# Three-product latent keys and values, and a weight unit shared between two engines inside the norms

## The chip, the core and the metric

One core of a Trainium2 chip runs the whole program. The metric is the device time of one execution in microseconds. In one core, TensorE (PE) multiplies, with its weight loads shown as PEld; VectorE (DVE), ScalarE (ACT) and GpSimd (POOL) work elementwise; SyncE (SP) issues most DMAs. PE writes PSUM, which has eight banks of 128 x 512 floats here; POOL works on SBUF alone.

## The reference

512 tokens of width 1024 pass through two layers of a first block and then one layer of a second block, all in float32. A layer of the first block projects x with `w_in` and mixes three groups: a gated recurrence, latent attention and attention to a memory. The latent group is

```
q = (_rmsnorm(cq, q_norm) @ w_uq).reshape(B, S, MLA_HEADS, MLA_NOPE + MLA_ROPE)
c = _rmsnorm(ckv, kv_norm)
k_nope = (c @ w_uk).reshape(B, S, MLA_HEADS, MLA_NOPE)
v = (c @ w_uv).reshape(B, S, MLA_HEADS, MLA_VDIM)
k_rope = _rope(kr, cos, sin)
```

with c of 512 x 128 and `w_uk`, `w_uv` of 128 x 512. The layer ends with `x = _layernorm(DEEPNORM_ALPHA * x + y, ln_g[l], ln_b[l])`. The second block is a chain of branches, each of the form `h = h + rms_norm(f(rms_norm(h, pre_g)), post_g)`: a feed-forward (SwiGLU, width 2816), a mixer (neighbourhood attention and pooling), a second feed-forward, and a last gated projection. Where one branch ends and the next begins, an outer norm and the next inner norm follow each other.

## The kernel before

**Split products.** Nearly every matrix product in float32 is made as three products of the shorter type `fp32r`. A factor w is split into `wh` (the high part, a cast to fp32r) and `wl = w - wh` (the low part), and PE adds `wh*xh`, `wh*xl` and `wl*xh` in one PSUM bank (L882 to L884).

**Units.** The weights come in 128-row tiles, four tiles to a unit. A `Block` of eight tiles has two units, and its pieces (unit, bank j) are PE's work, in this order: unit 0 with banks 0 to 3, then unit 1 with banks 0 to 3. For a unit, SP loads `raw` (two buffers, L812), ACT casts each tile to `wh` (three buffers, L1226, in `prepare`), and POOL subtracts to `wl` (L831). `low_on_dve(u, k)` says which tiles DVE subtracts instead (L1631, in `low`): every second one of the first eight units. SP loads a unit when the low parts of the unit two before are made. ACT casts a unit when its load has landed and PE is done with the unit three before. PE waits for tile k's low part at each unit's bank 0.

**Norms.** `norm_order` writes out by hand the order of each engine's steps over the four token tiles t, for the five norms between blocks. Four have an inner gain (`pre`) too: behind layer 1 of the first block (mode `layer`), behind the first feed-forward, the mixer and the second feed-forward (mode `post`). In these, per tile: the last partial products are added by DVE (`evac`; L1610), the outer gain is multiplied in (`gain`, L1952 or L1948), ACT makes the mean square and its root (`root`, L1491 and L1492), DVE finishes x (`x`, L1963 or L1960), ACT makes the second mean square and root (`root2`, L1498 and L1499), DVE multiplies by its reciprocal and by the inner gain in two halves (`n`, L1971), PE transposes the tile (`turn`, L1128), ACT casts it (`high`, L1509, or L1506 behind the first feed-forward), and DVE subtracts (`low`, L1987 or L1981). PE fills its time with the last pieces of the branch (`part`) and, from the first two transposed tiles, with the first halves of the next block's pieces: `early[0]`, transposes of tile 2, `early[1]`, transposes of tile 3, `early[2]`. `lots` cuts these pieces in three: for a block of eight such pieces 2, 4, 2 in mode `post` and 4, 2, 2 in mode `layer`; behind the second feed-forward there are four pieces (full width, half of the banks), cut 1, 2, 1. `early[0]` waits for `high(1)` and `low(1)`. ACT's casts of the next block's units stand in its order as `units`: unit 0 at the start of the norm, unit 1, all four tiles, behind `root2(2)` and before `root(3)` in mode `post` (behind `root2(2)` in mode `layer` too).

**Latent part.** `latent_norm` normalizes cq and ckv; `latent_turn` transposes them (L961), and ACT writes the high part `ch` of the queries' input, the whole c (`c_t`) and the rotary key (L1348 to L1352); DVE writes the low part of the queries' input (L1776). Behind it PE makes what is left of a gate block and the two blocks of `w_uq`, whose outputs DVE takes with L1596, and then the keys (L970) and values (L976): per layer four products each of plain float32, 128 x 128 by 128 x 512. ACT copies half of each key bank (L1368), then spreads the rotary key over the second half of the heads (L1362, L1363), and PE's first attention score (L991) waits for it. `w_uk` and `w_uv` are loaded whole beforehand.

Of the kernel before, what the change touches and what calls it, by code (L numbers as in the profile page):

```python
# [220 lines left out]
def norm_order(first, pre, turned):  # L221
# [9 lines left out]
    else:  # L231
# [17 lines left out]
        if first == "layer":  # L249
# [13 lines left out]
            def root(t):  # L263
# [5 lines left out]
            dve += [n(3), low(2), low(3)] if pre else [low(2), low(3)]  # L269
            act = [root(0), root2(0), [("units", 0)], root(1), high(0), root2(1), root(2), high(1), root2(2),  # L270
                   [("units", 1)], root(3), root2(3), high(2), high(3)]
        else:
            pe = parts[:5] + [turn(0), parts[5], parts[6], turn(1), parts[7], early[0], turn(2), early[1], turn(3), early[2]]
            act, dve = [[("units", 0)]], []
            for t in range(T):
# [13 lines left out]
    free = ("part", "early", "evac", "units")  # L289
# [4 lines left out]
def build(nc, x, x_t, mem_t, positions, w_in, w_uq, w_uk, w_uv, w_mk, w_mv, w_out, ln_g, ln_b, cols_in,  # L294
# [3 lines left out]
    with ctx:  # L298
# [24 lines left out]
        with nc.sbuf_tensor("work", [P, work_n], F32) as work:  # L323
            pass
        work2 = sb("work2", [P, work2_n])
# [35 lines left out]
        c_t, uk, uv = area(4224, 512), area(4736, 512), area(5248, 512)  # L361
# [100 lines left out]
        for l in range(DEPTH):  # L462
# [57 lines left out]
            add(latent_turn)  # L520
            add(between)
# [199 lines left out]

        def low_on_dve(u, k):

            return u < 8 and k % 2 == 1
# [111 lines left out]
        def _(pe):  # L836
# [63 lines left out]
            for e in plan:  # L900
# [67 lines left out]
                elif e.kind == "latent_keys":  # L968
                    for p in range(4):
                        pe.matmul(ps[:, 4 + p, :], uk[:, p * P:(p + 1) * P], c_t, start=True, stop=True).then_inc(pe_step, 1)  # L970
                elif e.kind == "latent_values":
                    for t in range(T):
# [3 lines left out]
                        pe.matmul(ps[:, 4 + t, :], c_t[:, t * P:(t + 1) * P], uv, start=True, stop=True).then_inc(pe_step, 1)  # L976
# [120 lines left out]
                elif e.kind == "norm":  # L1097
# [4 lines left out]
                    lots = early[:first], early[first:3 * n], early[3 * n:]  # L1102
# [83 lines left out]
        def _(act):  # L1186
# [23 lines left out]
            def prepare(pc, whole=False):  # L1210
# [4 lines left out]
                share = -(-units[last][2] * (j + 1) // b.banks)  # L1215
# [50 lines left out]
            for e in plan:  # L1266
# [77 lines left out]
                elif e.kind == "latent_turn":  # L1344
                    for n in range(4):
# [3 lines left out]
                        elif n == 2:  # L1349
                            ins = act.activation(c_t, ps[:, 6, :], ACT.Copy, scale=col("kv_gain", e.layer))  # L1350
                        else:
                            ins = act.copy(k_rope, ps[:, 7, :])  # L1352
                        ins.then_inc(act_step, 1)
                elif e.kind == "rope_table":
# [110 lines left out]
                elif e.kind == "norm":  # L1465
# [699 lines left out]
```

## Time and profile before

| | us |
|---|---|
| median of 3 runs | 2126.18 |
| lowest and highest | 2125.7, 2127.97 |
| the profiled execution's own time | 2127.59 |
| its span, first to last instruction | 2125.8 |
| PE busy (share of the span) | 2093.5 (98%) |
| PE weight loads busy | 1736.8 (82%) |
| DVE busy | 900.6 (42%) |
| POOL busy | 884.2 (42%) |
| ACT busy | 788.8 (37%) |

A busy engine has an instruction in flight. Matmuls overlap, so PE's progress is read from the distance between their starts and not from the length of one. The granted TensorE clock is 0.999 of full speed over the span.

### The profile page before, as it was taken

Reading aid. Unit: us, or ns where it says so; the run is one execution under the profiler, and the core shown is the slowest. Engines: PE = TensorE matmul, PEld = TensorE weight load, DVE = VectorE, ACT = ScalarE, POOL = GpSimd, SP = SyncE. Lnnn points to the kernel's source line nnn. Section 1 sums busy time; section 2 is a strip of 40 time slices with the busy share of each in tenths; the row PEclk is TensorE's granted clock in tenths of the full one; section 3 lists DMA queues with packets and bytes.
Section 4 is the critical chain, followed back from the end, with each engine's and each line's share of the span. In section 5 each row is a group of like instructions: output and inputs, shape, how many; then the busy total and the mean of one; then the engine's idle time right before and its main releaser. Section 6 shows DMA issues by size and latency. Waiting matters only on the chain.

```text
span 2125.8 us, 33452 instructions
## 1 busy us (share of the span) xinstructions
PE 2093.5 (98%) x13804; PEld 1736.8 (82%) x13804; DVE 900.6 (42%) x1639; ACT 788.8 (37%) x1607; POOL 884.2 (42%) x688
## 2 busy tenths in 40 slices
PE   7999999999999999999999999999999999999998
PEld 7888887778978887778888888888888888888876
DVE  6273565535373565526432221533422612222264
ACT  4424335454423325555422222335423432222244
POOL 4643433232543434233454444343445345444433
PEclk9999999999999999999999999999999999999999
DMA  6522223122222223122242332242232233332222
GB/s 234 180 74 80 77 67 100 41 80 80 80 82 80 77 67 99 40 80 76 72 140 89 110 99 93 76 134 80 76 103 99 62 109 101 106 116 87 96 70 89
DMA packets 98680, 196.65 MB, mean 93 GB/s; under 512 B 3681, under 2 KB 12257, under 8 KB 98145
## 3 DMA queue, kind: packets, MB, share of 16 engines
q1 hardware_dynamic: 95072, 183.25, 26.4%
q10 hardware_dynamic: 3456, 11.27, 1.5%
q8 instruction: 109, 1.79, 0.3%
q14 instruction: 43, 0.34, 0.1%
HBM read 192.41 MB, written 2.10 MB: 91 GB/s over the span
## 4 chain that ended last, share of the span: by engine, by line
PE 62%; DVE 5%; ACT 1%; issue 0%; DVEq 0%
PE ps L882 19%; PE ps L883 19%; PE ps L884 19%; DVE work L1971 1%; DVE xs L1963 1%; PE ps L991 1%; DVE work L1952 1%; PE ps L1068 1%; PE ps L999 0%; PE ps L1008 0%; PE ps L1151 0%; DVE side L1610 0%; PE ps L1171 0%; ACT work L1498 0%; DVE xl L1987 0%
## 5 line engine op out<-in xcount | busy, mean ns | idle before, releaser
L831 POOL TENSOR_TENSOR wl<-raw,wh 128x512 fp32r<-128x512 f32 (+2 forms) x684 | 884.0, 1317 | 1216.7 <-ACT wh L1226 1207.1
L1226 ACT CAST wh<-raw 128x512 fp32r<-128x512 f32 (+2 forms) x692 | 380.3, 603 | 772.0 <-PE ps L884 667.8
L882 PE MATMUL ps<-xh,wh 128*128 128x512 f32 (+1 forms) x1376 | 514.0, 374 | 1.2 <-issue 1.2
L884 PE MATMUL ps<-xh,wl 128*128 128x512 f32 (+1 forms) x1376 | 508.9, 370 | 0.0
L883 PE MATMUL ps<-xl,wh 128*128 128x512 f32 (+1 forms) x1376 | 508.4, 369 | 0.0
L882 PEld LDWEIGHTS ps<-xh,wh 128*128 128x128 f32 x1376 | 259.3, 188 | 46.1 <-issue 3.9
L884 PEld LDWEIGHTS ps<-xh,wl 128*128 128x128 f32 x1376 | 259.0, 188 | 44.6
L883 PEld LDWEIGHTS ps<-xl,wh 128*128 128x128 f32 x1376 | 259.3, 188 | 42.1
L882 PE MATMUL ps<-wh,xh 128*128 128x512 f32 (+1 forms) x608 | 239.0, 393 | 0.2 <-issue 0.2
L884 PE MATMUL ps<-wh,xl 128*128 128x512 f32 (+1 forms) x608 | 234.3, 385 | 0.0
L883 PE MATMUL ps<-wl,xh 128*128 128x512 f32 (+1 forms) x608 | 234.3, 385 | 0.0
L882 PE MATMUL ps<-wh,yh 128*128 128x512 f32 x496 | 198.1, 399 | 2.3 <-POOL wl L831 2.2
L884 PE MATMUL ps<-wh,yl 128*128 128x512 f32 x496 | 193.5, 390 | 0.0
L883 PE MATMUL ps<-wl,yh 128*128 128x512 f32 x496 | 193.3, 390 | 0.0
L1614 DVE TENSOR_TENSOR work<-ps,work 128x512 f32<-128x512 f32 x44 | 30.3, 688 | 380.6 <-PE ps L884 380.6
L882 PEld LDWEIGHTS ps<-wh,xh 128*128 128x128 f32 x608 | 114.1, 188 | 22.7 <-issue 1.3
L884 PEld LDWEIGHTS ps<-wh,xl 128*128 128x128 f32 x608 | 114.1, 188 | 21.8
L883 PEld LDWEIGHTS ps<-wl,xh 128*128 128x128 f32 x608 | 114.2, 188 | 20.3 <-issue 0.2
L882 PEld LDWEIGHTS ps<-wh,yh 128*128 128x128 f32 x496 | 93.3, 188 | 22.8 <-issue 2.8
L884 PEld LDWEIGHTS ps<-wh,yl 128*128 128x128 f32 x496 | 93.1, 188 | 20.0
L883 PEld LDWEIGHTS ps<-wl,yh 128*128 128x128 f32 x496 | 93.2, 188 | 18.4
L1610 DVE TENSOR_TENSOR side<-side,ps 128x512 f32<-128x512 f32 x88 | 59.3, 686 | 106.0 <-PE ps L884 103.4
(261 smaller groups left out, 2430.6 us busy)
## 6 DMA issues: line engine op xcount, KB each, us to landing
raw<-w_in SPq DMA_DIRECT2D x58, 1024.0 KB, 5.2
raw<-w_out SPq DMA_DIRECT2D x20, 1024.0 KB, 5.1
raw<-f1g SPq DMA_DIRECT2D x10, 1024.0 KB, 5.1
raw<-f1u SPq DMA_DIRECT2D x10, 1024.0 KB, 5.1
raw<-f1d SPq DMA_DIRECT2D x10, 1024.0 KB, 5.0
raw<-f2g SPq DMA_DIRECT2D x10, 1024.0 KB, 5.1
raw<-f2u SPq DMA_DIRECT2D x10, 1024.0 KB, 5.1
raw<-f2d SPq DMA_DIRECT2D x10, 1024.0 KB, 5.1
```

Of the source, the lines that this page charges most:

```text
L831: pool.tensor_tensor(wl[s], raw[:, u % 2, k, 0:b.width], wh[s].bitcast(F32), ALU.subtract).then_inc(low_done, 1)
L882: pe.matmul(o, still[0], move[0], start=k0 + k == 0, stop=False)
L883: pe.matmul(o, still[0], move[1], start=False, stop=False)
L884: mm = pe.matmul(o, still[1], move[0], start=False, stop=k0 + k == b.ktiles - 1)
L991: mm = pe.matmul(ps[:, 4 + h, 0:width], q_heads[:, 2 * p + h, cut], k_heads[:, p, h, 0:width], start=True, stop=True)
L1068: mm = pe.matmul(ps[o:o + 32, 4 + h, at:at + n], K[:, h, own:own + 32], right, start=True, stop=True)
L1226: act.copy(wh[:, v % 3, k, 0:width], raw[:, v % 2, k, 0:width]).then_inc(high_done, 1)
L1610: ins = dve.tensor_copy(dst, src) if first else dve.tensor_tensor(dst, dst, src, ALU.add)
L1614: link(dve.tensor_tensor(tmp, src, SG[:, j, :], ALU.mult))
L1952: step_done(dve.tensor_tensor(normed[:, t, :], facc[:, t, :], gain2_b[:, 0, :], ALU.mult))
L1963: step_done(dve.scalar_tensor_tensor(out=xt, in0=normed[:, t, :], scalar=r, in1=xt, op0=ALU.mult, op1=ALU.add))
L1971: step_done(dve.scalar_tensor_tensor(out=dst, in0=xs[:, t, cut], scalar=stat[:, 28 + t:29 + t], in1=gain2_b[:, 1, cut] if e.gain == "work2 ...
```

## The change

In the four norms with an inner gain, the second unit of the next block is treated in halves. ACT casts tiles 0 and 1 behind `high(1)` and before `root2(2)`, and tiles 2 and 3 behind `root(3)`. The low parts of tiles 2 and 3 go from POOL to DVE, in its order as `unit_low`, behind `x(3)`; in mode `post`, `low(2)` goes from behind `x(3)` to behind `n(3)`. Where the next block has eight early pieces, they are cut 2, 3, 3 (`post`) or 3, 2, 3 (`layer`).

In the latent part, a step `latent_split` behind `latent_turn` splits c, `w_uk` and `w_uv`: ACT writes the high parts, DVE the low ones (`uk_l` and `uv_l` in place of the raw weights). Keys and values become three fp32r products each.

```
-            dve += [n(3), low(2), low(3)] if pre else [low(2), low(3)]
-            act = [root(0), root2(0), [("units", 0)], root(1), high(0), root2(1), root(2), high(1), root2(2),
-                   [("units", 1)], root(3), root2(3), high(2), high(3)]
+            if pre:
+                dve += [[("unit_low", 0)], n(3), low(2), low(3)]
+                act = [root(0), root2(0), [("units", 0)], root(1), high(0), root2(1), root(2), high(1), [("units", 1)],
+                       root2(2), root(3), [("units", 2)], root2(3), high(2), high(3)]
+            else:
+                dve += [low(2), low(3)]
+                act = [root(0), [("units", 0)], root(1), high(0), root(2), high(1), [("units", 2)], root(3), high(2),
+                       high(3)]
...
-                if t:
+                if 0 < t < last:
                     dve.append(low(t - 1))
-                act.append([("units", 1), ("root", t)] if t == last else [("root", t)])
+                act.append([("root", t)])
+                if t == last:
+                    act.append([("units", 2)])
                 if t:
                     act.append(high(t - 1))
+                if t == last - 1:
+                    act.append([("units", 1)])
                 act.append(root2(t))
-            dve += [n(last), low(last)]
+            dve += [[("unit_low", 0)], n(last), low(last - 1), low(last)]
...
+            add(Phase("latent_split", act=2, dve=3, layer=l, free_running=True))
...
-            return u < 8 and k % 2 == 1
+            return k % 2 == 1 if u < 8 else u in shared_lows and k >= 2
...
-                        pe.matmul(ps[:, 4 + p, :], uk[:, p * P:(p + 1) * P], c_t, start=True, stop=True).then_inc(pe_step, 1)
+                        cut = slice(p * P, (p + 1) * P)
+                        pe.matmul(ps[:, 4 + p, :], uk_h[:, cut], c_h, start=True, stop=False)
+                        pe.matmul(ps[:, 4 + p, :], uk_h[:, cut], c_l, start=False, stop=False)
+                        pe.matmul(ps[:, 4 + p, :], uk_l[:, cut], c_h, start=False, stop=True).then_inc(pe_step, 1)
...
-                        pe.matmul(ps[:, 4 + t, :], c_t[:, t * P:(t + 1) * P], uv, start=True, stop=True).then_inc(pe_step, 1)
+                        cut = slice(t * P, (t + 1) * P)
+                        pe.matmul(ps[:, 4 + t, :], c_h[:, cut], uv_h, start=True, stop=False)
+                        pe.matmul(ps[:, 4 + t, :], c_h[:, cut], uv_l, start=False, stop=False)
+                        pe.matmul(ps[:, 4 + t, :], c_l[:, cut], uv_h, start=False, stop=True).then_inc(pe_step, 1)
...
-                    lots = early[:first], early[first:3 * n], early[3 * n:]
+                    second = 3 * n
+                    if e.gain and n == 2:
+                        first, second = 3 if e.mode == "layer" else 2, 5
+                    lots = early[:first], early[first:second], early[second:]
...
-                            if t < len(e.slots[1]):
-                                prepare(e.slots[1][t], whole=True)
+                            if e.tiles and t == 1:
+                                prepare(e.slots[1][1], upto=2)
+                            elif t < 3:
+                                prepare(e.slots[1][min(t, 1)], whole=True)
...
+                elif e.kind == "latent_split":
+
+                    act.wait_ge(small_loaded, e.loads_before)
+                    act.wait_ge(pe_step, e.pe)
+                    act.copy(uk_h, uk).then_inc(act_step, 1)
+                    act.copy(uv_h, uv).then_inc(act_step, 1)
...
+                elif e.kind == "latent_split":
+
+                    dve.wait_ge(act_step, e.act - 1)
+                    step_done(dve.scalar_tensor_tensor(out=c_l, in0=ps[:, 6, :], scalar=col("kv_gain", e.layer),
+                                                       in1=c_h.bitcast(F32), op0=ALU.mult, op1=ALU.subtract))
+                    for n, (low_part, whole, high_part) in enumerate(((uk_l, uk, uk_h), (uv_l, uv, uv_h))):
+                        dve.wait_ge(act_step, e.act + n + 1)
+                        step_done(dve.tensor_tensor(low_part, whole, high_part.bitcast(F32), ALU.subtract))
...
+                        elif key[0] == "unit_low":
+                            for k in (2, 3):
+                                low(e.next_block.unit_ids[1], k)
```

## Rows read from the trace of the kernel before

**Rows 1.** The page: span, and busy time of each engine

```profile
span 2125.8 us, 33452 instructions
...
PE 2093.5 (98%) x13804; PEld 1736.8 (82%) x13804; DVE 900.6 (42%) x1639; ACT 788.8 (37%) x1607; POOL 884.2 (42%) x688
```

**Rows 2.** PE's waits, whole span: us in total, times, longest

```profile
PE ps L1128 <- DVE work L1971: 5.9, 8, 1.2
```

**Rows 3.** Timeline of PE, mixer's norm: start, length, idle before

```profile
1691.00 0.36 PE L882 MATMUL ps<-xh,wh 128*128 128x256 f32 x1 [0.35 <-issue]
...
1693.94 0.60 PE L1128 MATMUL ps<-ident,work 128*128 128x128 f32 x4
1695.39 0.66 PE L1128 MATMUL ps<-ident,work 128*128 128x128 f32 x4 [0.85 <-DVE work L1971]
1695.80 0.36 PE L882 MATMUL ps<-xh,wh 128*128 128x256 f32 x1
...
1702.35 1.32 PE L1128 MATMUL ps<-ident,work 128*128 128x128 f32 x8 [0.55 <-DVE work L1971]
1703.42 0.36 PE L882 MATMUL ps<-xh,wh 128*128 128x256 f32 x1
```

**Rows 4.** Timeline of DVE, the same stretch

```profile
1688.42 1.28 DVE L1963 SCALAR_TENSOR_TENSOR xs<-work,stat,xs 128x1024 f32<-128x1024 f32 x1
...
1692.33 3.01 DVE L1971 SCALAR_TENSOR_TENSOR work<-xs,stat,work 128x512 f32<-128x512 f32 x2
1695.26 2.29 DVE L1952 TENSOR_TENSOR work<-side,work 128x1024 f32<-128x1024 f32 x1
...
1697.66 2.13 DVE L1963 SCALAR_TENSOR_TENSOR xs<-work,stat,xs 128x1024 f32<-128x1024 f32 x1
...
1701.54 1.42 DVE L1971 SCALAR_TENSOR_TENSOR work<-xs,stat,work 128x512 f32<-128x512 f32 x2
```

**Rows 5.** Timeline of ACT, the same stretch

```profile
1687.29 1.22 ACT L1509 CAST xh<-ps 128x512 fp32r<-128x512 f32 x2 [0.25 <-PE ps L1128]
1689.74 1.06 ACT L1498 ACTIVATE work<-xs 128x1024 f32<-128x1024 f32 x1 [1.23 <-DVE xs L1963]
...
1691.12 2.17 ACT L1226 CAST wh<-raw 128x512 fp32r<-128x512 f32 x4
...
1699.83 1.06 ACT L1498 ACTIVATE work<-xs 128x1024 f32<-128x1024 f32 x1 [3.16 <-DVE xs L1963]
```

**Rows 6.** Timeline of POOL, the same stretch

```profile
1691.80 6.91 POOL L831 TENSOR_TENSOR wl<-raw,wh 128x512 fp32r<-128x512 f32 x4 [18.57 <-ACT wh L1226]
```

**Rows 7.** By line: ns minimum/median/maximum, first and last start

```profile
L1971 DVE SCALAR_TENSOR_TENSOR work<-xs,stat,work x24: 744/752/1771, 1374.8 to 2070.2; 128x512 f32<-128x512 f32 x24
...
L1631 DVE TENSOR_TENSOR wl<-raw,wh x16: 683/1344/1781, 7.0 to 52.7; 128x512 fp32r<-128x512 f32 x16
...
L831 POOL TENSOR_TENSOR wl<-raw,wh x684: 724/1292/3210, 6.6 to 2099.9; 128x512 fp32r<-128x512 f32 x155, 128x256 fp32r<-128x256 f32 x12, 128x416 fp32r<-128x416 f32 x4
```

**Rows 8.** Timelines of PE and of its loads, layer 1's latent part

```profile
841.88 0.39 PE L884 MATMUL ps<-zh,wl 128*128 128x512 f32 x1
842.11 3.59 PE L970 MATMUL ps<-work 128*128 128x512 f32 x8
845.54 3.60 PE L976 MATMUL ps<-work 128*128 128x512 f32 x8
848.97 0.61 PE L991 MATMUL ps<-work 128*128 128x128 f32 x4
...
848.54 0.19 PEld L991 LDWEIGHTS ps<-work 128*128 128x128 f32 x1 [0.24 <-ACT work L1363]
```

**Rows 9.** Timeline of ACT, the same stretch

```profile
845.74 0.58 ACT L1368 COPY work<-ps 64x512 f32<-64x512 f32 x1 [0.28 <-PE ps L970]
```

**Rows 10.** Timeline of ACT and DVE behind the latent transposes

```profile
827.07 0.65 ACT L1226 CAST wh<-raw 128x512 fp32r<-128x512 f32 x1
...
832.57 0.69 DVE L1596 TENSOR_TENSOR work<-ps,rope_table 128x512 f32<-128x512 f32 x1 [5.96 <-PE ps L884]
```

More of the change, by code:

```diff
@@ L279, in norm_order @@
                 dve.append([("gain", t), ("x", t)])
-                if t:
+                if 0 < t < last:
                     dve.append(low(t - 1))
-                act.append([("units", 1), ("root", t)] if t == last else [("root", t)])
+                act.append([("root", t)])
+                if t == last:
+                    act.append([("units", 2)])
                 if t:
                     act.append(high(t - 1))
+                if t == last - 1:
+                    act.append([("units", 1)])
                 act.append(root2(t))
-            dve += [n(last), low(last)]
+            dve += [[("unit_low", 0)], n(last), low(last - 1), low(last)]
             act.append(high(last))
         pe, act, dve = (sum(order, []) for order in (pe, act, dve))
-    free = ("part", "early", "evac", "units")
+    free = ("part", "early", "evac", "units", "unit_low")
     at = [{k: i + 1 for i, k in enumerate(k for k in order if k[0] not in free)} for order in (pe, act, dve)]
@@ L324, in build @@
             pass
+        with nc.sbuf_tensor("front", [P, 2560], F32):
+            with nc.sbuf_tensor("latent_parts", [P, 3, 512], F32R) as latent_parts:
+                with nc.sbuf_tensor("middle", [P, 128], F32):
+                    with nc.sbuf_tensor("latent_lows", [P, 3, 512], F32R) as latent_lows:
+                        pass
         work2 = sb("work2", [P, work2_n])
@@ L360, in build @@
         ch, cl = zh[:, 0:2, :], zh[:, 2:4, :]
-        c_t, uk, uv = area(4224, 512), area(4736, 512), area(5248, 512)
+        uk, uv = area(4736, 512), area(5248, 512)
+        c_l, uk_h, uv_h = (latent_parts[:, i, :] for i in range(3))
+        c_h, uk_l, uv_l = (latent_lows[:, i, :] for i in range(3))
         q_heads, k_heads, k_rope = area(6144, 8, 512), area(10496, 4, 2, 512), area(B, 512)
@@ L720, in build @@
                     written[e.writes] = tuple(step)
+        shared_lows = {e.next_block.unit_ids[1] for e in plan
+                       if isinstance(e, Phase) and e.kind == "norm" and e.tiles and e.gain}
         def low_on_dve(u, k):
-            return u < 8 and k % 2 == 1
+            return k % 2 == 1 if u < 8 else u in shared_lows and k >= 2
         low_at, low_upto, lows = {}, [(0, 0)], [0, 0]
@@ L1208, in _, with prepare @@
             ahead = [2, 0]
-            def prepare(pc, whole=False):
+            def prepare(pc, whole=False, upto=None):
                 b, unit, j = pc
@@ L1214, in prepare @@
                 last = min(u, len(units) - 1)
-                share = -(-units[last][2] * (j + 1) // b.banks)
+                share = upto or -(-units[last][2] * (j + 1) // b.banks)
                 while ahead[0] <= last:
@@ L1349, in _ @@
                         elif n == 2:
-                            ins = act.activation(c_t, ps[:, 6, :], ACT.Copy, scale=col("kv_gain", e.layer))
+                            ins = act.activation(c_h, ps[:, 6, :], ACT.Copy, scale=col("kv_gain", e.layer))
                         else:
```

## The prediction

> **What bounds the kernel now.** I read the page first: TensorE (PE) is busy 2093.5 of 2125.8 us [rows 1]. So a saving must be PE time, either matmuls that get shorter or stretches in which PE waits. The second view is who PE waits for. In the whole span its matmuls wait 5.9 us, in eight waits, for L1971, which makes the twice-normed tile that PE transposes next [rows 2]. The eight are two in each of the four norms with an inner gain. Third, the timeline of one of them, the norm behind the mixer, engine by engine. PE starts `early[0]` at 1691.00 and the first transpose of token tile 2 at 1693.94. The second one comes only at 1695.39, after 0.85 us idle. `early[1]` runs from 1695.80, and tile 3's transposes start at 1702.35 after 0.55 us idle [rows 3]. VectorE (DVE) shows why. Its L1971 pair takes 3.01 us at 1692.33 but 1.42 at 1701.54. The product L1952 takes 2.29 us and L1963 2.13 at 1697.66, while L1963 took 1.28 at 1688.42 [rows 4]. GpSimd (POOL) subtracts four low parts from 1691.80 for 6.91 us, exactly over these slow ones [rows 6], released by four casts of ScalarE (ACT) at 1691.12 [rows 5]. Over all its uses L1971 has a median of 752 ns and a maximum of 1771 [rows 7]. POOL and DVE delay each other when both read two operands from SBUF.
>
> For the latent part I read PE's timeline of layer 1. Keys (L970) start at 842.11 and values (L976) at 845.54, four plain f32 products each, and the first attention score follows at 848.97. A split product of the same 512 columns starts 0.23 us before its successor (841.88 to 842.11) [rows 8].
>
> **The norms, part by part** (times of the mixer's norm).
>
> ACT: of the four casts of the next block's second unit, two move ahead of `root2(2)`, two behind `root(3)`. The `high(1)` casts run from 1687.29 for 1.22 us and end at 1688.5; `root2(2)` began only at 1689.74, since it waits for L1963, which ends at 1689.70 [rows 4, 5]. Two casts cost 2 x 0.54 (2.17 over 4) = 1.1 us and end at 1689.6, so they are hidden in the idle time. The weight buffer that they overwrite is free once piece (3,0) is done, which stands before tile 1's transposes in PE's order and so before `high(1)`. Their load waits only for low parts of earlier units, and POOL has been idle for 18.57 us before 1691.80 [rows 6], so it landed long before. `root(3)` no longer has four casts ahead of it: it starts at about 1692.1, when tile 3 has been added, and ends at 1693.6 (a square and root take about 1.55 us: ACT starts at 1699.83, DVE's next pair at 1701.54 less a 0.2 us reciprocal [rows 4, 5]). The other two casts end at 1694.7, and DVE asks for them only after `x(3)`.
>
> POOL: two subtractions instead of four. In the trace it starts 0.68 us after the casts do (1691.12 to 1691.80), so now at about 1689.1, while L1963 still runs. Either it waits until 1689.70 and works to about 1692.3 (two at the median of 1292 ns [rows 7]), or L1963 is stretched. The fast L1963 of 1.28 us beside a slow one of 2.13 [rows 4] leaves at most 0.85 us for that. I take no stretch: the slow L1971 of 1771 ns is its 744 plus 1.03 us, one whole stay behind POOL and not twice the speed lost, so the one already running keeps its place [rows 7].
>
> The Trainium skill, "SBUF — State Buffer", section Terms, says of the port pair that both engines use that it is exclusive and held for the full instruction, and that the loser fully blocks and doesn't share bandwidth. By that, L1963 keeps 1.28 us and my sum stands; by a shared bandwidth it would be up to 0.85 us longer in each norm and 3.4 us would be lost. The steps of one size in the trace agree with the rule.
>
> DVE: `n(2)` runs 1692.33 to 1693.75 instead of to 1695.3, because POOL is done. L1952 then takes 1.2 and L1963 1.28 us: `x(3)` ends at 1696.5 instead of 1699.8. The two moved subtractions cost 683 ns each, the fast case of the same subtraction in L1631 [rows 7]: 1.4 us, ending at 1697.9. They lie inside the wait for `root2(3)`, 1.55 us, after which `n(3)` runs from 1698.3 to 1699.7. `low(2)` moves behind `n(3)` and costs nothing: its reader is the second half of the block, after `early[2]`. If POOL got in between, each would cost up to 1781 ns [rows 7], 3.6 us for both, and `n(3)` would be 2.0 us later.
>
> PE: `early[0]` keeps two of eight pieces and ends at 1693.94 as before; the second transposes of tile 2 find `n(2)` ready. Both halves take about 1.0 us (1702.35 to 1703.42 for tile 3, without a wait between). `early[1]` now has three pieces, 36 products at 0.12 us (24 took 1691.00 to 1693.94 [rows 3]), so 4.4 us, to 1699.4. Its third piece needs the second unit's low parts in turn: it starts at about 1697.9 and its third product group 0.7 us later, against DVE's 1697.2 and 1697.9 for these two. That fits narrowly. Tile 3's second half is ready at 1699.7, a wait of 0.2 or so; `early[2]` has three pieces from 1700.2 to 1704.6. Before, it had two from 1703.42 to 1706.4. That is 1.8 us less. The other norms differ in the count: behind layer 1 the split is 3, 2, 3 instead of 4, 2, 2, behind the second feed-forward it stays 1, 2, 1. Their waits are of the same size (5.9 over 4 = 1.48 each, here 0.85 + 0.55 = 1.40). I take 1.7 x 4 = 6.8 us. Bounds: from 5.9 less 4 x 0.3 left over = 4.7, to 4 x 2.0 = 8.0.
>
> **The latent products.** PE now does 24 split products per layer for 8 plain ones: 24 x 0.234 = 5.6 us against 848.97 - 842.11 = 6.86. That is 1.24 us per layer of PE alone. But the first score waits for ACT's last spread of the rotary key. That chain is: last key product, 0.20 us, the copy L1368 at 845.74 [rows 9], then two spreads. PE's load for the score was released by the second one (L1363) at 848.54 [rows 8], which is where PE arrived anyway, with values from 845.54 at 0.43 us a load. The chain shortens only by the keys' part, 3.43 - 12 x 0.234 = 0.62 us. So the load comes at 847.92, and without a queued product ahead of it the product follows in about 0.2 instead of 0.43 us, at 848.1: 0.85 us won per layer, 1.7 in two. Bounds 1.2 (0.62 x 2) and 2.5 (1.24 x 2).
>
> The Trainium skill, "FP8 and Floating Point Precision", section TensorE Precision Notes, has true FP32 as four passes. Three for four would take a quarter off 6.86, 1.7 us a layer, against 1.24 by the trace, where a plain product takes 0.86 and three split ones 0.70.
>
> The splitting itself: two ACT copies (0.54 each) behind L1352, and three DVE subtractions (0.7 each, up to 1.8 beside POOL). DVE then waits 5.96 us until 832.57 for PE, so even 5.3 us would be covered. ACT has the cast at 827.07 behind it, 1.1 us later; it belongs to the second block of w_uq, which PE reads behind the whole first one, whose first output DVE takes at 832.57, so it is covered too [rows 10]. No DMA is added: the raw weights are loaded as before.
>
> **Sum.** 6.8 + 1.7 = 8.5 us from the profiled execution's 2127.59. Its span is 2125.8 and some 1.8 us lie around it; the median is 2126.18, 1.4 us under the profiled one, and I set the prediction against the median: 2126.2 - 8.5 = 2117.7 us. Everything behind a norm is paced by PE, so the time won is not given back there; the loads behind the norms start as much earlier.
>
> **Rivals.**
> (a) DVE takes on what POOL loses: the moved subtractions come late (slow beside POOL, or `root2(3)` is sooner than thought). Then only the first waits of each norm go, some 0.8 us x 4, plus 1.7: 4.9 us, 2121.3. For it: 1.4 us in a gap of 1.55 is tight. Against: POOL has nothing left to do there.
> (b) POOL's earlier start stretches L1963, and `low(1)`, on which `early[0]` waits at 1691.00, comes late by up to 0.85 us: 3.4 us lost, 5.1 won, 2121.1.
> (c) The latent part gains the full PE time or nothing, at 2116.9 or 2119.4: inside the range.
> (d) The other side: `early[1]` now holds a piece that needs the low parts which DVE makes last, behind `x(3)`, and `n(3)` stands behind them in the same queue. Each microsecond by which these are late beyond about 0.2 is paid by PE in all four norms. At 2.1 us late the norms' gain is gone; at 3.4 us late the kernel is 4 x 3.2 - 8.5 = 4.3 us slower, 2130.5. What would do it: casts held up in ACT's queue behind `root(3)`. Against: 1.8 us lie between the casts' end and `x(3)`.
> (e) It does nothing, since the waits are replaced by others one step on (`low(3)` before the second half): 2124.5 with the latent part alone. Against: `low(3)` gets 4.4 us of cover instead of 2.9.
>
> **Chances.** My forecast with (c) 0.70, (a) 0.09, (b) 0.09, (e) 0.08, (d) 0.04. A change of 0.2% is 4.25 us, about what a measurement of this kernel can tell from none. Faster by more: 0.70 + most of (a) and (b), 0.86; within: 0.11; slower: 0.03. The range reaches from 2115.7 (8.0 + 2.5) to 2121.9, which takes in (a) and (b).
>
> **What the profile of the changed kernel would show.** L1971 without any instance near 1771 ns in the norms, and at most 0.3 us of PE waits on it per norm; L1963 of tile 2 at 1.28 us (1.6 or more speaks for (b)); two subtractions of 0.68 us on DVE between `x(3)` and `n(3)`; keys at 2.8 us and values at 2.8 us, the score's load released by ACT's spread. PE waits on low parts inside `early[1]` would make (d) or (a) right and me wrong.

## The result and the profile after

The changed kernel takes 2114.88 us (median of 4 runs, 2114.51 to 2117.76), beside 2126.24 us (4 runs) for the kernel before on the same chip: a ratio of 0.9943, interval 0.9931 to 0.9955. The forecast was 2117.7 us with a range of 2115.7 to 2121.9. The direction was right. The gain is 11.4 us where 8.5 were forecast, and the time lies 0.8 us below the range.

The page of the changed kernel (span, busy time of each engine), and PE's waits over the whole span (us in total, times, longest):

```profile
span 2113.3 us, 33496 instructions
...
PE 2089.2 (99%) x13820; PEld 1741.6 (82%) x13820; DVE 894.8 (42%) x1653; ACT 789.8 (37%) x1611; POOL 868.0 (41%) x680
```

```profile
PE ps L902 <- POOL wl L851: 8.6, 2, 7.9
PE ps L1094 <- DVE work L1943: 2.6, 2, 1.3
PE ps L902 <- issue: 1.4, 4, 0.4
```

The eight waits for the twice-normed tile [rows 2] are gone altogether. PE's busy time went from 2093.5 us [rows 1] to 2089.2. Of these 4.3 us the latent parts gave 2.3. Up to the gated recurrence of layer 0 PE was 0.8 us busier, and most of the rest is time in which PE had stood still in the norms inside rows that count as busy (shown below). (In the changed kernel L902 to L904 are the split products, L1157 the norm's transposes, L2019 the twice-normed tile, L2000 the gain product, L2011 what `x` makes, L851 and L1668 the low parts on POOL and DVE, L1255 the weight casts.)

The mixer's norm on PE (start, length, then the idle time before, if any). It answers to [rows 3]:

```profile
1682.90 0.35 PE L902 MATMUL ps<-xh,wh 128*128 128x256 f32 x1 [0.35 <-issue]
...
1685.85 1.03 PE L1157 MATMUL ps<-ident,work 128*128 128x128 f32 x8
1686.64 0.36 PE L902 MATMUL ps<-xh,wh 128*128 128x256 f32 x1
...
1691.03 1.03 PE L1157 MATMUL ps<-ident,work 128*128 128x128 f32 x8
1691.82 0.36 PE L902 MATMUL ps<-xh,wh 128*128 128x256 f32 x1
```

Eight transposes now run as one row of 1.03 us, and the next product starts 0.79 us behind their start. Before, tile 2's were torn into 0.60, a wait and 0.66, and tile 3's came late and had a length of 1.32, with the next product 1.07 us behind their start. The same stretch on DVE, to be read beside [rows 4]:

```profile
1680.32 1.28 DVE L2011 SCALAR_TENSOR_TENSOR xs<-work,stat,xs 128x1024 f32<-128x1024 f32 x1
...
1684.23 1.41 DVE L2019 SCALAR_TENSOR_TENSOR work<-xs,stat,work 128x512 f32<-128x512 f32 x2
1685.56 1.22 DVE L2000 TENSOR_TENSOR work<-side,work 128x1024 f32<-128x1024 f32 x1
...
1686.89 1.28 DVE L2011 SCALAR_TENSOR_TENSOR xs<-work,stat,xs 128x1024 f32<-128x1024 f32 x1
1688.09 1.29 DVE L1668 TENSOR_TENSOR wl<-raw,wh 128x512 fp32r<-128x512 f32 x2
1689.72 0.17 DVE L2017 RECIPROCAL stat<-stat 128x1 f32<-128x1 f32 x1 [0.34 <-ACT stat L1536]
1689.92 1.41 DVE L2019 SCALAR_TENSOR_TENSOR work<-xs,stat,work 128x512 f32<-128x512 f32 x2
```

and on ACT and POOL, to be read beside [rows 5, 6]:

```profile
1680.31 1.14 ACT L1255 CAST wh<-raw 128x512 fp32r<-128x512 f32 x2
...
1685.41 1.12 ACT L1255 CAST wh<-raw 128x512 fp32r<-128x512 f32 x2
```

```profile
1681.01 3.01 POOL L851 TENSOR_TENSOR wl<-raw,wh 128x512 fp32r<-128x512 f32 x2 [15.53 <-ACT wh L1255]
```

The slow pair of L1971 (3.01 us) is now 1.41, the gain product 1.22 instead of 2.29, the second L2011 1.28 instead of 2.13. POOL starts its two at 1681.01, while the first L2011 runs; that one keeps its 1.28 us, and POOL has done at 1684.02, just ahead of L2019 at 1684.23. The two subtractions on DVE take 1.29 us and end 0.34 us before the root that `n(3)` waits for arrives.

The latent part of layer 1 on PE and on its weight loads, beside [rows 8]. Keys are L991 to L993, values L1000 to L1002, the score L1017:

```profile
841.86 0.39 PE L993 MATMUL ps<-latent_lows 128*128 128x512 f32 x1
842.08 0.39 PE L1000 MATMUL ps<-latent_parts,latent_lows 128*128 128x512 f32 x1
...
844.58 0.39 PE L1002 MATMUL ps<-latent_parts 128*128 128x512 f32 x1
845.06 0.71 PE L1017 MATMUL ps<-work 128*128 128x128 f32 x4
845.53 0.48 PE L902 MATMUL ps<-wh,yh 128*128 128x512 f32 x1
```

```profile
845.06 0.52 PEld L1017 LDWEIGHTS ps<-work 128*128 128x128 f32 x4 [0.52 <-ACT work L1398]
```

Each split product stands 0.227 us behind the one before. Between the last value product and the score lie 0.48 us, and PE's load waited 0.52 us for ACT's second spread (L1398). From the first key product (839.36) to the product behind the score it is now 6.17 us; before it was 7.23 (842.11 to 849.34).

**Where the time came from, by stages.** Starts of the same instruction in both profiled executions (2127.59 and 2115.07 us, 12.5 us apart):

- Up to the first matmul of the gated recurrence in layer 0 (line L1068 before, L1094 after; the "first level matmul" from here on), 106.36 before and 104.56 after: 1.8 us. Nothing of the change runs before it. The experiments below have this start anywhere from 104.31 to 107.83, so this is no part of the gain.
- The latent parts: 1.06 us in layer 1 and 0.95 in layer 0 (here from its first key product to layer 1's: 361.54 to 842.11 before, 359.74 to 839.36 now), 2.0 together. Up to the product behind the score layer 0 gains 1.06 too; 0.11 goes again between there and layer 1.
- The norms. From `early[0]`'s first product to the first behind tile 3's transposes it was 1691.00 to 1703.42, 12.42 us, and now it is 1682.90 to 1691.82, 8.92. One piece of 12 products (1.44 us) has moved behind that point, so the gain is 3.50 - 1.44 = 2.06 us. The same sum gives 2.06 behind layer 1 and 1.90 behind the first feed-forward; behind the second, where the cut didn't change, it is 2.42 outright. Together 8.4 us.

- Between the first feed-forward's norm and the mixer's: 0.38 us (1399.14 to 1691.00 before, 1389.98 to 1682.90 less the piece of 1.44 now). Of this, 0.35 lie at one place, the transposes of tile 0 in the mixer's norm. They start 0.43 us behind PE's last product, where it is 0.23 now, and the next product comes 0.98 us behind their start, where it is 0.83. DVE was late with the tile: its reciprocal before the tile began 0.45 us behind the end of ACT's root, and now begins 0.10 behind it. The other stretches give 0.1 back.

Behind the start-up that makes 10.7 us. The 11.4 between the medians are 0.7 more.

### The profile page after: what moved, and what is told of

Same layout as the page of the kernel before. It is cut to its first block, busy times and chain, and to the rows that moved or that the text cites. A ratio compares the mean times of both kernels' runs of the same rounds, so it can differ in the third digit from the quotient of the medians.

```text
span 2113.3 us, 33496 instructions
## 1 busy us (share of the span) xinstructions
PE 2089.2 (99%) x13820; PEld 1741.6 (82%) x13820; DVE 894.8 (42%) x1653; ACT 789.8 (37%) x1611; POOL 868.0 (41%) x680
## 4 chain that ended last, share of the span: by engine, by line
PE 59%; ACT 1%; DVE 0%; issue 0%; DVEq 0%
PE ps L902 18%; PE ps L903 18%; PE ps L904 18%; PE ps L1017 1%; PE ps L1157 1%; PE ps L1025 0%; PE ps L1034 0%; PE ps L1180 0%; PE ps L1200 0%; PE ps L1189 0%; PE ps L1070 0%; PE ps L1052 0%; ACT L1581 0%; PE ps L974 0%; PE ps L1210 0%; PE ps L1062 0%
## 5 line engine op out<-in xcount | busy, mean ns | idle before, releaser
L851 POOL TENSOR_TENSOR wl<-raw,wh 128x512 fp32r<-128x512 f32 (+2 forms) x676 | 867.8, 1307 | 1220.6 <-ACT wh L1255 1210.8
L1255 ACT CAST wh<-raw 128x512 fp32r<-128x512 f32 (+2 forms) x692 | 380.7, 604 | 773.3 <-PE ps L904 672.8
L902 PE MATMUL ps<-xh,wh 128*128 128x512 f32 (+1 forms) x1376 | 514.2, 374 | 1.2 <-issue 1.2
L904 PE MATMUL ps<-xh,wl 128*128 128x512 f32 (+1 forms) x1376 | 509.1, 370 | 0.0
L902 PEld LDWEIGHTS ps<-xh,wh 128*128 128x128 f32 x1376 | 259.4, 189 | 46.1 <-issue 3.9
L904 PEld LDWEIGHTS ps<-xh,wl 128*128 128x128 f32 x1376 | 259.1, 188 | 44.6
L902 PE MATMUL ps<-wh,xh 128*128 128x512 f32 (+1 forms) x608 | 239.1, 393 | 0.2 <-issue 0.2
L904 PE MATMUL ps<-wh,xl 128*128 128x512 f32 (+1 forms) x608 | 234.4, 386 | 0.0
L902 PE MATMUL ps<-wh,yh 128*128 128x512 f32 x496 | 198.0, 399 | 0.2
L904 PE MATMUL ps<-wh,yl 128*128 128x512 f32 x496 | 193.6, 390 | 0.0
L902 PEld LDWEIGHTS ps<-wh,xh 128*128 128x128 f32 x608 | 114.2, 188 | 22.6 <-issue 1.4
L904 PEld LDWEIGHTS ps<-wh,xl 128*128 128x128 f32 x608 | 114.2, 188 | 21.8
L902 PEld LDWEIGHTS ps<-wh,yh 128*128 128x128 f32 x496 | 93.3, 188 | 20.5 <-POOL wl L851 0.8
L904 PEld LDWEIGHTS ps<-wh,yl 128*128 128x128 f32 x496 | 93.1, 188 | 19.9
```

The lines of the kernel that those rows point to most:

```text
L851: pool.tensor_tensor(wl[s], raw[:, u % 2, k, 0:b.width], wh[s].bitcast(F32), ALU.subtract).then_inc(low_done, 1)
L902: pe.matmul(o, still[0], move[0], start=k0 + k == 0, stop=False)
L904: mm = pe.matmul(o, still[1], move[0], start=False, stop=k0 + k == b.ktiles - 1)
L1255: act.copy(wh[:, v % 3, k, 0:width], raw[:, v % 2, k, 0:width]).then_inc(high_done, 1)
```

## The experiments

Because the start-up varies by more than some of the questions, each kernel is read in two ways: by its median against the kernel before, and by the **time behind the start-up**, that is, the profiled execution's time less the start of its first level matmul. For before this is 2127.59 - 106.36 = 2021.23 us, for the changed kernel 2115.07 - 104.56 = 2010.51. The last column is the difference to 2021.23. What the column can't take off is a change of the granted clock behind the start-up, which matters for e5.

| kernel | median us | ratio to before (interval) | profiled - start | behind the start-up |
|---|---|---|---|---|
| changed | 2114.88 | 0.9943 (0.9931 to 0.9955) | 2115.07 - 104.56 | -10.7 |
| e8, changed again | 2115.45 | 0.9947 (0.9934 to 0.9959) | 2116.08 - 105.43 | -10.6 |
| e1, norms alone | 2118.93 | 0.9959 (0.9945 to 0.9972) | 2118.93 - 105.88 | -8.2 |
| e2, latent part alone | 2124.57 | 0.9988 (0.9979 to 0.9997) | 2123.49 - 104.45 | -2.2 |
| e3, casts moved, POOL keeps its low parts | 2120.06 | 0.9964 (0.9952 to 0.9977) | 2121.62 - 107.31 | -6.9 |
| e4, low parts shared, casts in the old place | 2121.18 | 0.9971 (0.9961 to 0.9982) | 2122.32 - 105.94 | -4.9 |
| e5, spread ahead of the keys | 2121.57 | 0.9975 (0.9966 to 0.9984) | 2124.63 - 107.83 | -4.4 |
| e6, old cut of the early pieces | 2115.45 | 0.9951 (0.9938 to 0.9964) | 2115.28 - 104.31 | -10.3 |
| e7, all four low parts on DVE | 2117.58 | 0.9957 (0.9943 to 0.9971) | 2118.49 - 105.71 | -8.5 |
| e9, spread pair by pair | 2114.01 | 0.9940 (0.9926 to 0.9953) | 2114.40 - 104.64 | -11.5 |
| e10, e9's edit on before | 2128.41 | 1.0004 (0.9995 to 1.0014) | 2128.56 - 107.44 | -0.1 |

The kernel before had medians of 2127.1 us beside e1 to e4, 2126.47 beside e5 to e8 and 2126.09 beside e9 and e10. e8 says what the last column is good to: 0.1 to 0.2 us for one and the same code, while the starts of the two profiles differ by 0.87.

**e1 and e2: the two halves of the change apart.** e1 has the norms as changed and the keys and values as plain products, with their splitting taken out. e2 is the reverse.

> The change without its latent part: keys and values are plain f32 products again. Theory: all that PE waited in the four norms is gone, 2.06 + 1.90 + 2.06 + 2.42 = 8.4 us by the starts in the two traces, so about 2117.8 us. Rival (the prediction's own term): the norms give 6.8 us and the rest came from elsewhere, 2119.4.

> The latent part alone, norms as before. Theory: 1.0 us less in each layer, 2.0 in all, 2124.2 us; keys to first score takes 5.9 us instead of 6.86, the last 0.5 of it a wait for the rotary spread. Rival: the first stage of the program, where the changed kernel's trace was 1.8 us ahead, belongs to the change (another memory layout), then 3.5 us or more, 2122.7.

Measured: 8.2 and 2.2 us behind the start-up, together 10.4 of 10.7. The halves add up, and the norms are the one that was underrated: e1 fits the 8.4 by starts and not the rival's 6.8. In e2, against its rival, what lies behind the start-up is 2.2 us and not 3.5. PE's waits in e2 still have the row of before, to the digit:

```profile
PE ps L1145 <- DVE work L2005: 5.9, 8, 1.2
```

So 5.9 us of waits stand there, and taking them away brings 8.2 to 8.4. PE's waits in this table don't hold the whole stall. The same table has them once more as the weight loads see them (the kernel before):

```profile
PEld ps L1128 <- DVE work L1971: 9.4, 15, 1.4
```

In the changed kernel's trace 0.4 us of these 9.4 are left, in two waits at tile 1 of the mixer's norm. A load takes its wait where it happens. PE's idle time is counted only from the end of the last product's row, and that row is 0.28 us long where the next product could follow in 0.12.

**e3 and e4: which of the two moves does it.** e3 leaves the casts where the change puts them and gives the two low parts back to POOL:

```
-            return k % 2 == 1 if u < 8 else u in shared_lows and k >= 2
+            return u < 8 and k % 2 == 1
```

e4 keeps DVE's share and puts the four casts back together (and the same for the norm behind layer 1):

```
-                act.append([("root", t)])
-                if t == last:
-                    act.append([("units", 2)])
+                act.append([("units", 2), ("root", t)] if t == last else [("root", t)])
...
-                if t == last - 1:
-                    act.append([("units", 1)])
```

> The changed kernel, but POOL makes all four low parts of the second unit; ACT's order stays as changed. Theory (the two engines block each other at SBUF): POOL's third low part starts before x(3) and x(3) waits for it, n(3) is 0.9 us later in each norm, 3.6 us in all, 2118.5 us. Rival (all of the gain is that ACT's casts no longer stand ahead of root(3)): as the changed kernel, 2114.9.

> The changed kernel, but ACT casts all four tiles behind root2(2) and before root(3), as before; DVE still makes two low parts. Theory: POOL's two low parts start 2.7 us later and fall on n(2), and root(3) is 1.0 us later, so the first wait of each norm comes back, some 0.9 to 1.5 us each, 2118.5 to 2121 us. Rival (only the number of low parts on POOL counts): as the changed kernel, 2114.9.

Measured behind the start-up: e3 loses 3.8 us of the change's 10.7, e4 loses 5.8. With the 2.2 us of the latent part taken off, the casts' place alone is worth 4.7 us, DVE's share alone 2.7, both 8.4: they add up to a little less than the whole. In e3 it is tile 3's stall that comes back, in three of the four norms (behind the second feed-forward PE doesn't wait). POOL's second pair falls on `x(3)` (timelines of DVE and POOL, mixer's norm), and PE waits for the tile:

```profile
1692.21 2.13 DVE L2010 SCALAR_TENSOR_TENSOR xs<-work,stat,xs 128x1024 f32<-128x1024 f32 x1
...
1696.08 1.42 DVE L2018 SCALAR_TENSOR_TENSOR work<-xs,stat,work 128x512 f32<-128x512 f32 x2
```

```profile
1691.42 4.08 POOL L851 TENSOR_TENSOR wl<-raw,wh 128x512 fp32r<-128x512 f32 x2 [2.09 <-ACT wh L1255]
```

In e4 tile 2's stall comes back in all four norms. The four casts run as a block at 1687.46, POOL starts its two at 1688.14, just ahead of the twice-normed tile, and this is 3.01 us long again (timelines of DVE and PE):

```profile
1688.66 3.01 DVE L2015 SCALAR_TENSOR_TENSOR work<-xs,stat,work 128x512 f32<-128x512 f32 x2
```

```profile
1691.73 0.66 PE L1153 MATMUL ps<-ident,work 128*128 128x128 f32 x4 [0.84 <-DVE work L2015]
...
1696.42 0.28 PE L900 MATMUL ps<-xh,wl 128*128 128x256 f32 x1
1696.76 1.32 PE L1153 MATMUL ps<-ident,work 128*128 128x128 f32 x8
1697.83 0.36 PE L898 MATMUL ps<-xh,wh 128*128 128x256 f32 x1
```

A smaller part of tile 3's stall is back too, in three norms. Here it is 0.22 us ahead of the transposes (0.34 behind the last product instead of 0.12) and 0.28 inside them, since the late tile 2 makes tile 3 late. So each half of the move takes away mainly one stall, and the two are not quite independent. The slow gain product of before (2.29 us) comes back in neither: POOL's two subtractions are over when it starts (1.22 us in e3, 1.21 in e4).

**e6 and e8: is the new cut of the early pieces worth anything?** e6 is the changed kernel with the old cut, and e8 the changed kernel again.

```
-                    second = 3 * n
-                    if e.gain and n == 2:
-                        first, second = 3 if e.mode == "layer" else 2, 5
-                    lots = early[:first], early[first:second], early[second:]
+                    lots = early[:first], early[first:3 * n], early[3 * n:]
```

> The changed kernel with the early pieces cut as before (2, 4, 2 and 4, 2, 2). Theory: n(3) is ready 0.1 us ahead of the end of a three-piece early[1]; with four pieces it is ready sooner still, and what is lost is only cover for low(3) behind the last transposes, 2.9 us against about 2.1 needed: no difference, 2114.9. Behind layer 1, early[0] with four pieces hides more, so none is lost there either. Rival: the new cut is part of the gain, 0.3 us or more a norm, 2116.

> The changed kernel itself, beside the others on the same chip: a ratio near 0.9943 to the kernel before. Its first 104 us tell how far the start of the program differs by itself from one execution to the next.

Both have a median of 2115.45 us, and e6 is 0.3 us behind e8 by the last column, hardly more than that column's own error. The cut gives nothing that can be measured. Its third piece of `early[1]`, on which rival (d) rested, never waited in any norm of the changed kernel.

**e7: does DVE have room for all four low parts?**

```
-            return k % 2 == 1 if u < 8 else u in shared_lows and k >= 2
+            return k % 2 == 1 if u < 8 else u in shared_lows
...
-                            for k in (2, 3):
+                            for k in range(4):
```

> The changed kernel, but DVE makes all four low parts of the second unit, all between x(3) and n(3). Theory: two fit into the 1.55 us for which DVE waits for root2(3); the other two delay n(3) by 1.2 us, and PE pays about 1.0 of it in each norm: 4 us, 2119. Rival: with POOL wholly out of the norms some SBUF collision that is left goes too, and it comes out even or better.

A loss, as expected, but of 2.3 us and not 4. DVE's four take 2.49 us, 1.20 more than two. Of that 0.34 falls into DVE's old wait for the root, and `n(3)` starts 7.78 us behind `early[0]` instead of 7.02, 0.76 later. PE pays for it in three of the four norms, 0.5, 0.7 and 0.7 us; behind the second feed-forward it doesn't wait. Timelines of DVE and of PE, mixer's norm:

```profile
1690.38 2.49 DVE L1668 TENSOR_TENSOR wl<-raw,wh 128x512 fp32r<-128x512 f32 x4
```

```profile
1693.79 1.32 PE L1157 MATMUL ps<-ident,work 128*128 128x128 f32 x8 [0.24 <-DVE work L2019]
1694.86 0.36 PE L902 MATMUL ps<-xh,wh 128*128 128x256 f32 x1
```

These two rows show where my forecast went short. The wait is shown as 0.24 us, but the next product is 1.07 us behind the transposes' start instead of 0.79: 0.28 us more stand inside the row, whose length is 1.32 instead of 1.03. A tile has two halves, and the second one is waited for as well.

**e5: the spread of the rotary key ahead of the keys.** The last spread (L1397, L1398) is queued on ACT before the key copies instead of behind them, so that the score needn't wait for it.

```
+            spread = Phase("rope_spread", act=1, free_running=True, group=0)
+            spread.behind = plan[-1]
+            add(spread)
             add(keys)
             add(values)
-            add(Phase("rope_spread", act=1, free_running=True, group=0))
...
+                    if e.group == 0:
+                        act.wait_ge(bank_ready, e.behind.ready[3])
```

> The changed kernel, with the second spread of the rotary key ahead of ACT's key copies; ACT waits for the last query block to be done, since the spread overwrites its input. Theory: in each layer the 0.5 us that PE waits for the spread goes, less some 0.1 to 0.2 for key copies that now come later: 0.7 us in all, a ratio of 0.9997 to the changed kernel, within noise by the clock but plain in the trace (last value product to first score 0.23 to 0.3 us instead of 0.48). Rival: the copies are late for the values, and PE waits as long there.

The expectation of the time failed: 6.3 us lost. The edit made a new wait which I had overlooked. PE's key step waits for every ACT step queued before it, and now the spread is one of them (timeline of PE, layer 1, the first key product and the way from the last value product to the score):

```profile
848.85 0.50 PE L993 MATMUL ps<-latent_lows,latent_parts 128*128 128x512 f32 x1 [2.24 <-ACT work L1402]
...
854.20 0.39 PE L1004 MATMUL ps<-latent_parts 128*128 128x512 f32 x1
854.43 0.60 PE L1019 MATMUL ps<-work 128*128 128x128 f32 x4
```

The spread itself can't start before the second block of w_uq is through, whose operand lies in the buffer that it writes. The first key product comes 2.64 us behind the product before it instead of 0.23, so this wait costs 2.4 us in each layer, 4.8 in all. In layer 0 there is more: the granted clock is 0.50, the 1.2 GHz level, from 366.47 to 369.88 us, 1.0 us behind the end of PE's wait, and the stretch from the first key product to the product behind the score takes 7.55 us where layer 1's takes 5.94. The 1.6 us between them are about what 3.41 us at half the clock cost, by an estimate of 3.41 / 2 = 1.7. The sign in the trace did come: with the spread done early the score follows the last value product in 0.23 us instead of 0.48. So the theory of the gap is borne out, and its rival, late copies for the values, isn't seen; what failed is the price, since a wait was put on a phase's whole past.

**e9 and e10: the spread pair by pair, in the changed kernel and in the one before.** This is e5's question asked properly: the order stays, but the first score waits for pair 0's copies only.

```
-            add(Phase("rope_spread", act=1, free_running=True, group=0))
+            add(Phase("rope_spread", act=2, free_running=True, group=0))
...
-                    wait(pe, act_step, e.act)
+                    wait(pe, act_step, e.act - 1)
...
+                            if k == 4:
+                                pe.wait_ge(act_step, e.act)
...
-                    pairs = slice(2 * e.group, 2 * e.group + 2)
                     act.wait_ge(act_step, e.act)
...
+                    for pairs in (slice(2, 4),) if e.group else (slice(0, 1), slice(1, 2)):
```

> The changed kernel, but the last spread of the rotary key is made pair by pair (four copies of 64x512 instead of two of 64x1024), and the first score waits for pair 0 alone; the product for pair 1 waits for the rest. Theory: in the changed kernel the latent part is no longer bound by PE but by ACT's chain (key copies, then two spreads), which costs the first score 0.25 us per layer: the last value product starts at 844.58 and the score at 845.06, where 0.23 would follow a pitch. With pair 0 ready some 1.1 us sooner the score follows the last value product in 0.23 to 0.3 us, without a wait on ACT: from the first key product to the first product behind the score 5.9 us instead of 6.17, in all 0.4 to 0.6 us won, about 2114.9 us by the median of the changed kernel. Rival: the gap is PE's own (loading the score's weights behind a value product), then it stays at 0.48 us and the time is that of the changed kernel.

> The same edit on the kernel before. Theory: there the plain value products end last and ACT's spread just meets them, so the score starts where it did (8 plain products from the first key product, 6.86 us) and nothing is won: 0 to 0.2 us. Rival: if ACT's chain had been the bound before as well, the score would start up to 0.4 us sooner per layer, and the gain of the three-product form would have been measured against a late start.

PE's timeline of e9, layer 1, from the first key product on:

```profile
839.12 0.39 PE L991 MATMUL ps<-latent_lows,latent_parts 128*128 128x512 f32 x1
...
844.33 0.39 PE L1002 MATMUL ps<-latent_parts 128*128 128x512 f32 x1
844.56 0.61 PE L1019 MATMUL ps<-work 128*128 128x128 f32 x4
844.92 0.48 PE L902 MATMUL ps<-wh,yh 128*128 128x512 f32 x1
```

The score now follows the last value product in 0.23 us instead of 0.48, and its own row is 0.61 long instead of 0.71, as in [rows 8]: behind a wait it had been longer. So the rival, a gap of PE's own, is out. From the first key product to the product behind the score it is 5.80 us, where the changed kernel has 6.17. That is 0.37 us per layer, and 0.75 by the last column. The time is 2114.01 us (2113.93 to 2114.46, 5 runs), the fastest of the study; against the changed kernel the two ratio intervals overlap, and it is the stage that shows the difference.

In e10 the score comes 6.87 us behind the first key product, as before. So before the change PE's plain products bound that place and ACT's chain just met them; with the change ACT's chain bounds it, and e9 takes that away. One of e10's ten runs took 5402.8 us, for which nothing here gives a reason. The other nine spread from 2125.7 to 2128.9, those of before beside it from 2125.5 to 2128.6, and the start-up of its profile is one of the latest (107.44). The median in the table is that of all ten.

## Why the prediction was right in kind and short in size

**The stalls and what made them: right.** The slow L1971, the slow gain product and the slow L1963 were all POOL's four subtractions. They are gone at the places named. e4 brings back the slow L1971 and e3 the slow L1963. The slow gain product is shown by the timelines alone, since POOL's subtractions lie beside it in neither.

**POOL's earlier start: right.** I chose no stretch for the first L1963, against up to 0.85 us, rival (b). It took 1.28, and POOL, two of whose subtractions would take 2.58 us by its median of 1292 ns [rows 7], needed 3.01. The one already running kept its place and the later one waited. The Trainium skill says so ("SBUF — State Buffer", Terms: the pair of ports is exclusive and the loser fully blocks), and this trace agrees: a shared bandwidth would have made L2011 longer too. My "one whole stay" was loose, though: the 1.03 us by which the slowest L1971 was longer is less than a POOL subtraction of 1.29, and in the mixer's norm the first of the slow pair took 1.32 us and the second 1.77.

**DVE's share: right.** 1.29 us for the two against 1.4, inside the wait for the root, with 0.34 us to spare where I had some 0.15. Rival (a) did not come about; e7 shows how near it was: 1.2 us more work on DVE in each norm costs 2.3 us in all.

**The size of the norms' gain: this is the step that failed.** "Both halves take about 1.0 us (1702.35 to 1703.42 for tile 3, without a wait between)". There was a wait between. A turn that finds its tile ready has the next product 0.79 us behind its start; tile 3's turn of before has 1.07. The merged row shows the wait for its first half in brackets and hides that for its second. The weight loads of the same transposes show it (before, timeline of PEld):

```profile
1702.35 0.42 PEld L1128 LDWEIGHTS ps<-ident,work 128*128 128x128 f32 x4 [0.75 <-DVE work L1971]
1703.01 0.42 PEld L1128 LDWEIGHTS ps<-ident,work 128*128 128x128 f32 x4 [0.24 <-DVE work L1971]
```

With tile 2's 1.09 the loads' waits in this norm are 2.08 us for these two tiles. Done by PE's starts, a norm of before holds three pieces of stall:

- tile 2's turn, 1693.94 to 1695.80, less 0.79: 1.07 us, where the waits have 0.85;
- tile 3's turn, 1702.35 to 1703.42, less 0.79: 0.28 us, where the waits have none;
- ahead of tile 3's turn: from 1695.80 to 1702.35 it is 6.55 us for four pieces, which without a wait take 4.39 (three, 1686.64 to 1691.03) + 1.44 = 5.83: 0.72 us, where the waits have 0.55.

The sum is 2.07 us, and 2.06 were won. My working let tile 2's turn end at 1695.0, 1.06 us behind its start, where 0.79 is right: 0.27 us in each norm, 1.1 of the 1.6 missing. I then took 1.7 for the 1.8 that it gave, to keep nearer to the waits of 1.40: another 0.3. So the term that was mis-sized is the 6.8 us of the norms, and it measured 8.4. The yardstick stood in the trace of before. Its turn for tile 0 in the first feed-forward's norm is one undisturbed row on PE's timeline:

```profile
1376.08 1.04 PE L1128 MATMUL ps<-ident,work 128*128 128x128 f32 x8
1376.87 0.48 PE L882 MATMUL ps<-wh,zh 128*128 128x512 f32 x1
```

**"A wait of 0.2 or so" for tile 3's second half: it did not come.** I had `n(3)` 7.3 us behind `early[0]`'s start (1698.3 - 1691.00); it began 7.0 behind it (1689.92 - 1682.90). The turn at 1691.03 then has no wait, and the next product follows in 0.79 us, as my 1699.4 to 1700.2 had it with the wait.

**Scaling from one norm: low for the second feed-forward.** I took 1.7 x 4. That norm had the longest waits (0.95 and 0.81), and gave 2.42. My upper bound of 8.0 was 4 x 2.0, and 8.4 lies above it.

**The latent part: mechanism right, size low.** ACT's chain is the new bound, as forecast, and PE's load waits for L1398. I had 0.85 us per layer and it is 0.95 and 1.06. Two terms were off. The first is "24 x 0.234": a split product here stands 0.227 us behind the last, so keys and values take 5.45 us, and the load for the score comes 5.70 us behind the first key product instead of 6.43, a gain of 0.73 (845.06 - 839.36, 848.54 - 842.11) where I had 0.62. The second is the "about 0.2" from that load to its product: they now start together (both at 845.06), which gives 0.43 where I had 0.23. The score's own row gives 0.10 of it back. Together 1.06, as measured in layer 1. PE's own gain, of which rival (c) spoke, is larger too: e9 reaches the score in 5.44 us where it took 6.86, 1.42 us a layer for my 1.24. The Trainium skill has four passes for true FP32 ("FP8 and Floating Point Precision", TensorE Precision Notes); the estimate from that was 1.7 us a layer. The runs give a ratio of 5.45 to 6.86, 0.79 and not 0.75.

**The sum.** 8.5 us forecast, 10.7 measured behind the start-up: of the 2.2 missing 1.6 are the norms, 0.3 the latent parts and 0.3 stretches that the change doesn't touch. Between the medians another 0.7 us is added, which is of the size of the start-up's variation and can't be told from it.

**Left open.** Why DVE began 0.45 us behind ACT's root at tile 0 of the mixer's norm. It did so in the kernel before and in e10, and 0.10 behind it in the ten kernels that have either half of the change, though none of the edits touches that step. And why PE's wait at 48 us in the start-up varies (below).

## What to carry to other kernels

Size a stall by the starts of the work behind it, against an undisturbed copy of the same step in the same trace, and not by PE's waits as the profile prints them. They held 5.9 us of 8.4 here: a wait between two halves of a merged row doesn't show, and the others are counted from the end of the last row and not from where the next product could have started. The waits of the weight loads (9.4 us) came nearer. When two engines hold each other up, look at both the time and the engine of the work: moving the casts alone kept 4.7 us and sharing the subtractions alone 2.7. And stop when the receiving queue's gap is full, as four subtractions in a gap for two lost 2.3 us. When PE's work shrinks, look at who arrives second: a copy chain that just met the old end is the next bound, and letting the first consumer wait only for what it needs gave 0.75 us more.

## What the runs showed of the hardware

- The first 105 us vary: the first level matmul started between 104.31 and 107.83 us in twelve profiled executions, though the edits touch nothing that runs before it. Most of it lies in one wait of PE for a low part, which ends at 46 to 48 us: none that shows in the changed kernel's trace, 0.24 us in e6, 2.25 before, 2.45 in e5. In the three latest (e3, e5, e10) the granted clock was 0.50, the 1.2 GHz level, for 3.4 us right behind this wait, and the products of 512 columns there started 0.43 us apart instead of 0.23. In the kernel before and in e4 the clock stayed at the 2.4 GHz level behind waits of 2.25 and 2.12 us. With the start-up taken off, equal code agrees to 0.1 to 0.2 us.
- A plain f32 product of 512 columns took 0.86 us (6.86 over 8), a split one 0.227, so three of them 0.68.
- Behind a wait the next start is late as well, but only by a little. The second product of a waited score group came 0.21 us behind the first (0.11 without a wait), that of waited transposes 0.16 us (0.11 without).
- POOL's subtraction and DVE's instructions with two operands in SBUF held each other up whole: L2011 kept 1.28 us and POOL's two took 3.01 instead of 2.58. DVE's subtractions with one operand in PSUM (L2035, beside POOL's at 1681.52) kept their 1.28 us for two.
